# Block inverses in two pairs of groups with one transpose in, and a gated feed-forward whose norm factor is applied at the PSUM read

## The chip, the cores and the metric

One Trainium2 chip, one of its cores, one launch. The metric is the device time of that launch in microseconds (us). The core has TensorE (PE) for matrix products, VectorE (DVE), ScalarE (ACT), GpSimd (POOL) and SyncE (SP, which here only issues DMAs). All data is float32; products are done in float32 or, for the large weights, as three products of rounded parts (below).

## The reference, cut to what matters

256 tokens of width 1024 pass through two layers of a first block and one layer of a second one. A layer of the first block is

```python
x = x + 0.5 * swiglu(rms_norm(x, ffn1_norm[l]), ffn1_w_in[l], ffn1_w_out[l])
... mixer: forgetting attention, RWKV-7, block attention, then mix_w_out
... cross attention to a memory
x = x + 0.5 * swiglu(rms_norm(x, ffn2_norm[l]), ffn2_w_in[l], ffn2_w_out[l])

def rms_norm(t, g):  y = t * rsqrt(mean(t * t, -1) + 1e-6);  return y * g
def swiglu(h, w_in, w_out):
    gate, up = split(h @ w_in, 2, -1);  return (silu(gate) * up) @ w_out
```

with w_in 1024 x 5632 and w_out 2816 x 1024. So there are four gated feed-forwards. The factor rsqrt(...) is one number a token, the gain g one a feature.

RWKV-7 and, in the second block, the gated delta rule (GDN, 8 heads, two directions, chunks of 64 tokens) each need the inverse of unit triangular 64 x 64 matrices: 16 units of 128 rows (two matrices each) at a time, once in each layer's RWKV and once in each of GDN's four quarters (direction x half of the heads). In GDN the 64 x 64 inverses are joined to the units that the scan uses.

## The kernel before, in words

**Stages.** The kernel is a row of blocks; each engine has its own program in a block, and all meet at its end. Activations lie feature-major: tile k of 8 holds 128 features by 256 tokens.

**Slabs.** Weights come in slabs of 1 MB (8 x 128 rows by 256 columns) through a ring of three places; SP issues a slab's DMA when the slab three before it is no longer needed (`load_slabs`, L267). `Split` (L326 to L379) makes a rounded part `slab_hi` on ACT (L354) and the rest `slab_lo` on POOL (L363), in three places each: ACT may start slab i when PE is done with slab i-3; POOL follows ACT; PE waits for `slab_lo`. `product3` (L382) then gives hi x hi, hi x lo and lo x hi, so that a slab is 48 matmuls of 256 columns.

**Feed-forward** (`ffn_stage`, L519). The norm (`Norm`, L440) comes first: ACT squares x (L464), PE sums over features with a matrix of ones, 8 float32 matmuls (L484), ACT takes the root as Ln and Exp (L470, L472; each loads a table), DVE makes h = x * gain * rstd (L491), ACT and DVE split h (L420, L426), and only then PE starts on slab 0. Meanwhile PE runs four idle products (`keep_busy`, L433). In the first feed-forward of a layer the gain comes by a DMA that SP issues behind the first three slabs (`LayerParams`, L781). Then 11 pairs of slabs: slab 2i gives 256 gate columns into one bank, slab 2i+1 the up columns into another; ACT applies Silu out of PSUM (L555), DVE multiplies with the up bank (L593), ACT and DVE split the product (L558, L426). Before w_out (12 slabs, L502) PE waits for the last product, since its first sums go to banks 0 and 1, which the last pair (i = 10) also uses.

```python
for jj in range(4):
    if jj >= 2:
        pe.wait_ge(x_updated, 2 * (jj - 1))
    ... K.bank[2 * (jj % 2) + j]
```

**Inverse** (`BlockSolve` L1192, `Inverse` L1279). DVE turns the 32-row diagonal strips of the matrices with four transposes, each of 32 partitions by 512 (L1219), inverts 16 x 16 blocks on all partitions at once (L1222 to L1248), ACT widens the result for X (L1266, four instructions) while POOL widens it for its transpose xt (L1269, four), DVE turns both back (L1253, 1024 columns each). Then two levels join 16-blocks to 32 and 64: with M the masked part (POOL, L1326), T = M X (PE), T is copied to SBUF (ACT, L1395), U = xt T and V = T xt (PE), X -= U, xt -= V (DVE, L1409, L1410). The 16 units go in four groups of 4 units (256 columns); groups 0 and 1 run all their levels, then groups 2 and 3, each group of a pair with two banks (U goes over T). In GDN a third level joins the halves (L1355, L1371, L1414, L1415). ACT copies the diagonal blocks of each group before the solve (L1383).

**GDN** (`gdn_stages`, L2922). In quarter q the inverse of q and the scan of q-1 are interleaved by hand: scan steps 0 to 3 with the matrices, 4 to 7 with the solve, step 8 + pair ahead of each pair of inverse steps (six pairs).

## Time and profile before

| | us |
|---|---|
| median of 3 runs | 2930.77 (2929.78 to 2937.19) |
| the profiled execution | 2935.89 |
| its span | 2934.0 |
| mean granted TensorE clock of it | 0.888 |

| engine | busy, share of the span |
|---|---|
| PE | 2444.5 (83%) |
| DVE | 1165.4 (40%) |
| ACT | 1122.3 (38%) |
| POOL | 1242.2 (42%) |

An engine's busy share says how much of the span its instructions cover; matmuls overlap, so that PE's share is not its share of peak. What a stage costs is read from the waits inside it: who is idle, and what ends the idle time. The granted clock is 1.0 at 2.4 GHz and 0.5 at 1.2 GHz.

### The profile page before, as it was taken

How to read it: one execution, taken by the hardware profiler on the slowest of the kernel's cores; microseconds unless marked ns; L12 is line 12 of the kernel's file. 1: busy time of each engine (PE TensorE's matmuls, PEld its weight loads, DVE VectorE, ACT ScalarE, POOL GpSimd, SP SyncE). 2: the span in 40 equal slices, each digit the busy share in tenths (PEclk: the TensorE clock that was granted, in tenths of full speed). 3: DMA queues.
4: the chain of work that ended last, by engine and by line, in shares of the span. 5: the costliest groups of instructions: out<-in, count | busy, mean ns of one | idle time of the engine just before them, and what ended most of it. 6: DMA issues, size and time to landing. Idle time of an engine off the chain costs nothing. (4 is left out here: it accounts for less than half of the span.)

```text
span 2934.0 us, 42793 instructions
## 1 busy us (share of the span) xinstructions
PE 2444.5 (83%) x18163; PEld 2122.1 (72%) x18163; DVE 1165.4 (40%) x2067; ACT 1122.3 (38%) x1495; POOL 1242.2 (42%) x356
## 2 busy tenths in 40 slices
PE   5998968877898998977967899699957776887878
PEld 4997845375898998854456799567746556787878
DVE  2112664332210111665242211266756664334990
ACT  4433422434442443322334443456832221533333
POOL 2874510051775775610033577332211110774655
PEclk8999968987999999977987999899967777898998
DMA  4554401431553553500333354321000000553432
GB/s 138 187 175 123 144 1 44 132 125 46 172 180 124 171 182 118 173 29 12 121 113 101 110 180 143 126 76 58 29 1 1 1 1 17 171 172 115 143 123 94
DMA packets 298691, 305.98 MB, mean 104 GB/s; under 512 B 7249, under 2 KB 294461, under 8 KB 298493
## 3 DMA queue, kind: packets, MB, share of 16 engines
q1 hardware_dynamic: 298493, 303.16, 32.1%
q8 instruction: 146, 2.39, 0.4%
q14 instruction: 52, 0.43, 0.0%
HBM read 302.09 MB, written 1.05 MB: 103 GB/s over the span
## 5 line engine op out<-in xcount | busy, mean ns | idle before, releaser
L363 POOL TENSOR_TENSOR slab_lo<-ring,slab_hi 128x2048 fp32r<-128x2048 f32 (+1 forms) x242 | 1096.5, 4540 | 1045.8 <-ACT slab_hi L354 1045.8
L354 ACT CAST slab_hi<-ring 128x2048 fp32r<-128x2048 f32 (+1 forms) x242 | 451.1, 1868 | 639.8 <-PE bank L386 573.4
L384 PE MATMUL bank<-ffn_h_hi,slab_hi 128*128 128x256 f32 x1408 | 403.1, 286 | 24.0 <-DVE ffn_h_lo L426 24.0
L385 PE MATMUL bank<-ffn_h_lo,slab_hi 128*128 128x256 f32 x1408 | 402.2, 286 | 0.0
L386 PE MATMUL bank<-ffn_h_hi,slab_lo 128*128 128x256 f32 x1408 | 402.1, 286 | 0.0
L384 PEld LDWEIGHTS bank<-ffn_h_hi,slab_hi 128*128 128x128 f32 x1408 | 274.5, 195 | 27.2 <-issue 27.2
L385 PEld LDWEIGHTS bank<-ffn_h_lo,slab_hi 128*128 128x128 f32 x1408 | 274.4, 195 | 0.0
L386 PEld LDWEIGHTS bank<-ffn_h_hi,slab_lo 128*128 128x128 f32 x1408 | 274.2, 195 | 0.0
L593 DVE TENSOR_TENSOR hidden<-gate,bank 128x512 f32<-128x512 f32 x44 | 30.2, 687 | 456.8 <-PE bank L386 456.8
L384 PE MATMUL bank<-ffn_hidden_hi,slab_hi 128*128 128x256 f32 x704 | 199.6, 284 | 3.3 <-DVE hidden L593 3.3
L385 PE MATMUL bank<-ffn_hidden_lo,slab_hi 128*128 128x256 f32 x704 | 199.2, 283 | 0.0
L386 PE MATMUL bank<-ffn_hidden_hi,slab_lo 128*128 128x256 f32 x704 | 199.2, 283 | 0.0
L1326 POOL TENSOR_TENSOR inv_m<-inv_d,const 128x256 f32<-128x256 f32 x48 | 34.4, 733 | 324.3 <-ACT inv_d L1383 273.1
L2259 POOL TENSOR_TENSOR tile_lo<-ring,tile_hi 128x1024 fp32r<-128x1024 f32 (+1 forms) x38 | 87.6, 2310 | 189.3 <-ACT tile_hi L2252 189.3
L384 PEld LDWEIGHTS bank<-ffn_hidden_hi,slab_hi 128*128 128x128 f32 x704 | 135.1, 192 | 4.2 <-DVE hidden L593 4.2
L386 PEld LDWEIGHTS bank<-ffn_hidden_hi,slab_lo 128*128 128x128 f32 x704 | 135.1, 192 | 0.0
L385 PEld LDWEIGHTS bank<-ffn_hidden_lo,slab_hi 128*128 128x128 f32 x704 | 135.1, 192 | 0.0
L384 PE MATMUL bank<-fh_hi,slab_hi 128*128 128x256 f32 x352 | 103.6, 294 | 32.4 <-POOL slab_lo L363 18.5
L3233 DVE SCALAR_TENSOR_TENSOR fcon<-fraw,prm,fcon 128x256 f32<-128x256 f32 x88 | 126.5, 1498 | 0.8
L2270 PE MATMUL bank<-both_hi,tile_hi 128*128 128x512 f32 (+2 forms) x296 | 107.8, 380 | 21.3 <-ACT tile_hi L2252 21.3
L385 PE MATMUL bank<-fh_lo,slab_hi 128*128 128x256 f32 x352 | 102.9, 292 | 0.0
L1668 PE MATMUL bank<-ring,cs 128*2 128x256 f32 x384 | 102.8, 394 | 0.0
(570 smaller groups left out, 5847.8 us busy)
## 6 DMA issues: line engine op xcount, KB each, us to landing
ring<-in_ffn_w_in SPq DMA_DIRECT2D x88, 1024.0 KB, 5.1
ring<-in_ffn_w_out SPq DMA_DIRECT2D x32, 1024.0 KB, 5.0
ring<-in_w_in SPq DMA_DIRECT2D x30, 1024.0 KB, 5.3
ring<-in_mix_w_in SPq DMA_DIRECT2D x24, 1024.0 KB, 5.4
...
```

What stands on the lines that cost most here:

```text
L354: act.copy(self.hi[i % self.PLACES][:, 0:w], K.ring[n % RING][:, 0:w]).then_inc(self.hi_ready, 1)
L363: pool.tensor_tensor(self.lo[i % self.PLACES][:, 0:w], place[:, 0:w], self.hi[i % self.PLACES][:, 0:w].bitcast(F32), ALU.subtract).then_in ...
L384: pe.matmul(out, w[0], act[0], start=start, stop=False)
L385: pe.matmul(out, w[0], act[1], start=False, stop=False)
L386: return pe.matmul(out, w[1], act[0], start=False, stop=stop)
L593: dve.tensor_tensor(whole_hidden[:, i % 2, :], gate[:, i % 2, :], K.bank[2 * (i % 2) + 1][:, :], ALU.mult).then_inc(product_ready, 1)
L1326: pool.tensor_tensor(self.mask[s][l % 2][:, :, :], self.diag[g][:, :, :], level, ALU.mult)\
L1668: last = pe.matmul(K.bank[self.BANKS[self.n % 2]][0:2, 0:HALF], K.cs[:, self.k, :], self.w[:, self.k, :], start=(self.k == 0), stop=(self. ...
L2259: last = pool.tensor_tensor(self.lo[u % self.PLACES][:, :, dst], self.source(u)[:, :, src], self.hi[u % self.PLACES][:, :, dst].bitcast(F3 ...
L2270: pe.matmul(out, hi[:, k, 0:m], both.hi[:, k, 0:tokens], start=(k == 0), stop=False)
L3233: last = dve.scalar_tensor_tensor(o[:, q, :], r[:, q, j:j + T], tap, o[:, q, :], ALU.mult, ALU.add)
```

## The change

Feed-forward: PE no longer waits for the norm. The parts are made from x * gain (without rstd), the sum of squares is built on DVE (squares of all 2048 columns, then three additions) and summed over partitions by one matmul after the second slab, and rstd is multiplied in when DVE reads the gate and up banks. PE starts on `slab_hi` alone and takes the `slab_lo` products after the others of the first half. The first gain DMA goes ahead of the slabs, with a tile of its own. POOL starts when all of x's parts are there. w_out's first sums go to banks 2 and 3 (in the convolutional feed-forward too).

```diff
+def feature_major_late(pe, split, bank, w, act, first=None):
+
+    for j in range(2):
+        out, col = bank[:, j * T:(j + 1) * T], slice(j * P, (j + 1) * P)
+        for k in range(KD):
+            if first is not None and j == 0:
+                first(k)
+            pe.matmul(out, w[0][:, k, col], act[0][:, k, :], start=(k == 0), stop=False)
+            pe.matmul(out, w[0][:, k, col], act[1][:, k, :], start=False, stop=False)
+        if j == 0:
+            split.wait_rest(pe)
+        for k in range(KD):
+            last = pe.matmul(out, w[1][:, k, col], act[0][:, k, :], start=False, stop=(k == KD - 1))
     return last
...
-def ffn_out_pe(K, pe, split, hidden, x_updated):
+def out_bank(jj, j):
+    return 2 * ((jj + 1) % 2) + j
+
+
+def ffn_out_pe(K, pe, split, hidden, x_updated, other_banks):
 
     for jj in range(4):
+        if jj == 1:
+            other_banks()
         if jj >= 2:
...
+    def act_parts(self, act):
+        for k in range(KD):
+            last = act.activation(self.parts.hi[:, k, :], self.x[:, k, :], ACT.Copy, scale=self.gain[:, k:k + 1])
+            if k % 2:
+                last.then_inc(self.parts.hi_ready, 1)
+
+    def act_root(self, act):
+        K = self.K
+        act.wait_ge(self.squared_summed_root, 2)
+        K.act_own.after(act, act.activation(self.rstd[:, :], self.bank[:, 0:T], ACT.Ln, bias=K.c("eps"), scale=1.0 / D))
+        act.activation(self.rstd[:, :], self.rstd[:, :], ACT.Exp, scale=-0.5).then_inc(self.squared_summed_root, 1)
+
+    def dve_parts(self, dve):
+        for k in range(KD):
+            if k % 2 == 0:
+                dve.wait_ge(self.parts.hi_ready, k // 2 + 1)
+            last = dve.scalar_tensor_tensor(self.parts.lo[:, k, :], self.x[:, k, :], self.gain[:, k:k + 1],
+                                            self.parts.hi[:, k, :].bitcast(F32), ALU.mult, ALU.subtract)
+            if k % 2:
+                last.then_inc(self.parts.lo_ready, 1)
+
+    def dve_squares(self, dve):
+
+        sq, own = self.K.h, self.K.dve_own
+        own.after(dve, dve.tensor_tensor(sq[:, :, :], self.x[:, :, :], self.x[:, :, :], ALU.mult))
+        for n in (4, 2):
+            own.after(dve, dve.tensor_tensor(sq[:, 0:n, :], sq[:, 0:n, :], sq[:, n:2 * n, :], ALU.add))
+        dve.tensor_tensor(sq[:, 0, :], sq[:, 0, :], sq[:, 1, :], ALU.add).then_inc(self.squared_summed_root, 1)
+
+    def pe(self, pe):
+        pe.wait_ge(self.squared_summed_root, 1)
+        pe.matmul(self.bank[:, 0:T], self.K.c("ones"), self.K.h[:, 0, :], start=True, stop=True).then_inc(self.squared_summed_root, 1)
...
             def _(pool):
+                pool.wait_ge(parts.lo_ready, KD // 2)
...
             def _(act):
-                norm.act(act, between=lambda: split.act(act, 2))
+                if params is not None:
+                    act.wait_ge(params.first_ready, 1)
+                else:
+                    split.act(act, 1)
+                norm.act_parts(act)
+                split.act(act, 3)
+                norm.act_root(act)
                 for i in range(N):
                     split.act(act, 2 * i + 4)
-                    K.wait_slabs(act, n0 + 2 * i + 1)
-                    if i >= 2:
-                        act.wait_ge(product_ready, i - 1)
-                    act.activation(gate[:, i % 2, :], K.bank[2 * (i % 2)][:, :], ACT.Silu).then_inc(silu_ready, 1)
+                    act.wait_ge(gate_ready, i + 1)
+                    act.activation(gate[:, i % 2, :, :], gate[:, i % 2, :, :], ACT.Silu).then_inc(silu_ready, 1)
                     split.act(act, 2 * i + 5)
                     act.wait_ge(product_ready, i + 1)
-                    act.copy(flat(hidden.hi[:, pair_of(i), :]), whole_hidden[:, i % 2, :]).then_inc(hidden.hi_ready, 1)
+                    hidden.act(act, pair_of(i), whole_hidden[:, i % 2, :, :])
...
-                norm.pe(pe)
                 if params is not None:
                     params.pe_first(pe)
-                keep_busy(K, pe, K.bank[5], 4)
+                keep_busy(K, pe, K.bank[4], 3)
...
                     for part in range(2):
-                        w = split.next_view(pe)
+                        w = split.next_rounded(pe)
                         if i >= 2:
                             pe.wait_ge(product_ready, i - 1)
-                        K.slab_done(feature_major3(pe, K.bank[2 * (i % 2) + part], w, (parts.hi, parts.lo), KD, HALF,
-                                                   first=(lambda k: pe.wait_ge(parts.lo_ready, k // 2 + 1))
-                                                   if i == part == 0 else None))
-                pe.wait_ge(product_ready, N)
-                ffn_out_pe(K, pe, split, hidden, x_updated)
+                        K.slab_done(feature_major_late(pe, split, K.bank[2 * (i % 2) + part], w, (parts.hi, parts.lo),
+                                                       first=(lambda k: pe.wait_ge(parts.lo_ready, k // 2 + 1))
+                                                       if i == part == 0 else None))
+                    if i == 0:
+                        norm.pe(pe)
+                pe.wait_ge(product_ready, N - 1)
+                ffn_out_pe(K, pe, split, hidden, x_updated, lambda: pe.wait_ge(product_ready, N))
...
                 if params is not None:
                     params.dve_first(dve)
-                norm.dve(dve)
+                norm.dve_parts(dve)
+                norm.dve_squares(dve)
+                dve.wait_ge(norm.squared_summed_root, 3)
...
                     if i < N:
+                        K.wait_slabs(dve, n0 + 2 * i + 1)
+                        if i >= 2:
+                            dve.wait_ge(product_ready, i - 1)
+                        dve.tensor_tensor(gate[:, i % 2, :, :], pair(2 * (i % 2)), norm.all_tokens(2), ALU.mult)\
+                            .then_inc(gate_ready, 1)
+                    if i >= 1:
+                        hidden.dve(dve, pair_of(i - 1), whole_hidden[:, (i - 1) % 2, :, :])
+                    if i < N:
+                        K.wait_slabs(dve, n0 + 2 * i + 2)
+                        if i >= 1:
+                            dve.wait_ge(product_ready, i)
+                        K.dve_own.after(dve, dve.tensor_tensor(up[:, :, :], pair(2 * (i % 2) + 1), norm.all_tokens(2),
+                                                               ALU.mult))
                         dve.wait_ge(silu_ready, i + 1)
-                        K.wait_slabs(dve, n0 + 2 * i + 2)
                         if i >= 2:
                             dve.wait_ge(hidden.lo_ready, i - 1)
-                        dve.tensor_tensor(whole_hidden[:, i % 2, :], gate[:, i % 2, :],
-                                          K.bank[2 * (i % 2) + 1][:, :], ALU.mult).then_inc(product_ready, 1)
-                    if i >= 1:
-                        hidden.dve(dve, pair_of(i - 1),
-                                   whole_hidden[:, (i - 1) % 2, :].rearrange("p (a t) -> p a t", a=2))
+                        dve.tensor_tensor(whole_hidden[:, i % 2, :, :], up[:, :, :], gate[:, i % 2, :, :], ALU.mult)\
+                            .then_inc(product_ready, 1)
```

`LayerParams.sync_first` issues the first gain DMA, `dve_first` now signals `first_ready`; `wait_rest` waits for `lo_ready` of the slab that `next_rounded` gave.

Inverse: ACT gathers the diagonal strips of each group into one 128 x 512 tile (`compact`), which DVE turns with one transpose; DVE widens for X, ACT for xt, POOL no longer takes part in that. The levels run over two pairs of groups (8 units, 512 columns), one level of each in turn, with three banks each; T1 and `compact` share space with the widened tiles.

```diff
+    def act_compact(self, act, g):
+
+        for i, rows in enumerate(self.GROUPS):
+            act.copy(self.p.compact[rows, 4 * g:4 * g + 4, :], self.lt[rows, 4 * g:4 * g + 4, 32 * i:32 * i + 32])\
+                .then_inc(self.compacted, 1)
...
-        for g, rows in enumerate(self.GROUPS):
-            src = self.lt[rows, :, 32 * g:32 * g + 32].rearrange("p u (b c) -> p c b u", b=2)
-            last = dve.transpose(p.turned[rows, :, :], src)
-        K.dve_own.after(dve, last)
+        dve.wait_ge(self.compacted, 16)
+        K.dve_own.after(dve, dve.transpose(p.turned[:, :, :], p.compact.rearrange("p u (b c) -> p c b u", b=2)))
...
+    def dve_out(self, dve):
+
+        K = self.K
+        dve.wait_ge(self.solved, 1)
+        K.dve_own.after(dve, self.widen(0, lambda out, src, scale: dve.tensor_scalar(out, src, scale, None, ALU.mult)))
+        for i, dst in enumerate(self.targets):
+            if i:
+                dve.wait_ge(self.widened, 1)
+            dve.transpose(dst[:, :, :].rearrange("p u (b c) -> p c b u", b=4),
+                          self.p.wide[i].rearrange("p c a r -> p (c a) r")).then_inc(self.x_ready, 1)
 
     def act(self, act):
-        self.widen(act, 0, lambda out, src, scale: act.activation(out, src, ACT.Copy, scale=scale))
-
-    def pool(self, pool):
-        self.widen(pool, 1, lambda out, src, scale: pool.tensor_scalar(out, src, scale, None, ALU.mult))
+
+        act.wait_ge(self.solved, 1)
+        self.widen(1, lambda out, src, scale: act.activation(out, src, ACT.Copy, scale=scale)).then_inc(self.widened, 1)
...
+        bank = K.bank[bank:bank + 6]
+        self.t_bank, self.u_bank, self.v_bank = bank[0:2], bank[2:4], bank[4:6]
...
+        self.steps = [(p, l) for l in self.levels for p in range(2)]
...
+    def pe_second(self, pe, i):
+        p, l = self.steps[i]
+        pe.wait_ge(self.t_copied, i + 1)
+        pe.wait_ge(self.x_ready, 2 if i < 2 else 2 + i - 1)
+        if l != self.JOIN:
+            if l != self.levels[-1]:
+                self.blocks(pe, self.u_bank[p], self.xt(p), self.T1[p])
+            last = self.blocks(pe, self.v_bank[p], self.T1[p], self.xt(p))
+        else:
+            src, dst = self.joined()
+            for q in range(8):
+                last = pe.matmul(self.v_bank[p][src, q * CH:(q + 1) * CH], self.T1[p][dst, q, :],
+                                 self.xt(p)[dst, q, :], start=True, stop=True)
+        last.then_inc(self.uv_ready, 1)
+
+    def pe(self, pe, between=lambda i: None):
+
+        self.pe_first(pe, 0)
+        self.pe_first(pe, 1)
+        for i in range(0, len(self.steps), 2):
+            for step in (i, i + 1):
+                self.pe_second(pe, step)
+                between(step)
+            if i + 2 < len(self.steps):
+                self.pe_first(pe, i + 2)
+                self.pe_first(pe, i + 3)
...
+            act.copy(self.diag[half, 4 * g:4 * g + 4, :], self.lt[half, 4 * g:4 * g + 4, half]).then_inc(self.d_ready, 1)
+        self.solve.act_compact(act, g)
```

With eight units an instruction, `blocks` issues 16 matmuls instead of 8, and ACT's and DVE's instructions have 512 columns instead of 256; POOL makes four masks of 512 columns instead of eight of 256 (RWKV and GDN). `gdn_stages` is unchanged, but `between` is now called after each of the six second halves, so scan step 8 + i stands behind U and V of inverse step i. In the scan, the product for the new state goes to bank 0 and the output to bank 1 alone, with a wait of the fourth output for the copy of the third.

## Rows read from the trace of the kernel before

**Rows 1.** The page: TensorE's granted clock in 40 equal slices of the span, in tenths.

```profile
PEclk8999968987999999977987999899967777898998
```

**Rows 2.** Busy time by stretch (from:to, length, PE, PEld, DVE, ACT, POOL, clock, DMA share, GB/s).

```profile
36.20:56.80 20.60, 12.56 (x25) 7.37 (x26) 6.56 (x12) 11.95 (x15) 8.97 (x2) 0.67 0.70 224
56.80:186.40 129.60, 129.58 (x1057) 129.46 (x1057) 15.06 (x23) 53.79 (x44) 100.62 (x22) 0.98 0.54 174
725.00:741.80 16.80, 7.15 (x24) 4.48 (x24) 7.47 (x10) 11.76 (x15) 8.99 (x2) 0.80 0.34 109
...
409.50:426.70 17.20, 0.00 (x0) 0.00 (x0) 12.62 (x27) 3.37 (x6) 3.63 (x4) 0.50 0.00 0
426.70:440.90 14.20, 12.89 (x320) 12.02 (x320) 6.48 (x14) 2.98 (x8) 2.90 (x4) 0.84 0.01 3
...
2185.50:2207.00 21.50, 18.45 (x448) 17.20 (x448) 10.44 (x25) 7.48 (x20) 2.87 (x4) 0.90 0.01 3
...
2312.00:2336.50 24.50, 7.38 (x32) 6.31 (x32) 17.93 (x45) 2.82 (x7) 6.11 (x7) 0.57 0.00 0
2336.50:2366.00 29.50, 26.98 (x504) 25.00 (x504) 15.31 (x40) 8.75 (x22) 2.95 (x4) 0.89 0.01 2
```

**Rows 3.** ACT in order of time, second feed-forward of layer 0: start, length, operation.

```profile
727.10 3.68 ACT L354 CAST slab_hi<-ring 128x2048 fp32r<-128x2048 f32 x2
...
732.09 0.47 ACT L470 ACTIVATE rstd<-bank,const 128x256 f32<-128x256 f32 x1
732.58 1.28 ACT L472 ACT_TABLE_LOAD   x1
733.88 0.42 ACT L472 ACTIVATE rstd<-rstd 128x256 f32<-128x256 f32 x1
```

**Rows 4.** PE in order of time there; then the first gain in the first feed-forward.

```profile
725.68 3.72 PE L484 MATMUL bank<-h,const 128*128 128x256 f32 x16 [2.36 <-ACT h L464]
729.24 3.60 PE L433 MATMUL bank<-const 128*128 128x512 f32 x8
741.85 0.55 PE L384 MATMUL bank<-ffn_h_hi,slab_hi 128*128 128x256 f32 x1 [9.01 <-DVE ffn_h_lo L426]
...
47.63 0.27 PE L827 MATMUL bank<-const,param_rows 8*128 8x8 f32 x1 [4.42 <-DMA param_rows<-in_ffn_norm]
```

**Rows 5.** Small DMAs of the mixer (L962, L964), issue to landing.

```profile
DMA to landing us min/median/max: 2.5/2.6/2.9
```

**Rows 6.** POOL and DVE in order of time, there; last, the first feed-forward's same product.

```profile
762.99 4.62 POOL L363 TENSOR_TENSOR slab_lo<-ring,slab_hi 128x2048 fp32r<-128x2048 f32 x1 [1.13 <-ACT slab_hi L354]
...
741.02 2.48 DVE L426 TENSOR_TENSOR ffn_h_lo<-h,ffn_h_hi 128x512 fp32r<-128x512 f32 x4
...
766.79 0.69 DVE L593 TENSOR_TENSOR hidden<-gate,bank 128x512 f32<-128x512 f32 x1 [10.83 <-PE bank L386]
...
82.79 0.69 DVE L593 TENSOR_TENSOR hidden<-gate,bank 128x512 f32<-128x512 f32 x1 [10.83 <-PE bank L386]
```

**Rows 7.** DVE, POOL and PE at the turn from w_in to w_out, first feed-forward.

```profile
188.58 3.59 DVE L426 TENSOR_TENSOR ffn_hidden_lo<-hidden,ffn_hidden_hi 128x512 fp32r<-128x512 f32 x1 [0.66 <-ACT ffn_hidden_hi L558]
...
188.10 3.52 POOL L363 TENSOR_TENSOR slab_lo<-ring,slab_hi 128x1536 fp32r<-128x1536 f32 x1 [0.73 <-ACT slab_hi L354]
...
187.30 0.39 PE L384 MATMUL bank<-ffn_hidden_hi,slab_hi 128*128 128x256 f32 x1 [0.84 <-DVE hidden L593]
```

**Rows 8.** DVE and ACT in the first GDN quarter's solve and first level.

```profile
2168.26 4.16 DVE L1219 STREAM_TRANSPOSE sol_turned<-ring 32x512 f32<-32x512 f32 x4
2172.45 0.35 DVE L1222 TENSOR_SCALAR sol_coef<-sol_turned,const 128x256 f32<-128x256 f32 x1
...
2183.48 1.93 DVE L1253 STREAM_TRANSPOSE inv_x<-sol_wide 128x1024 f32<-128x1024 f32 x1 [3.76 <-POOL sol_wide L1269]
...
2168.26 0.83 ACT L1383 COPY inv_d<-ring 64x256 f32<-64x256 f32 x2 [2.69 <-DVE ring L2784]
2179.76 2.57 ACT L1266 ACTIVATE sol_wide<-sol_solved,const 128x256 f32<-128x256 f32 x4 [10.67 <-DVE sol_solved L1248]
```

221 lines of the change are left out of this document (104 added, 117 removed).

## The prediction

> **What bounds the kernel now.** I first read the page's slices of the granted clock [rows 1]: they dip where the serial stages are, so I looked at both parts of the change by stretch [rows 2]. In the steady part of a feed-forward the reader is to see that PE is busy through 129.58 of 129.60 us at clock 0.98: 1057 matmuls, 22 slabs at about 5.8 us. POOL has 100.62 of work there, 4.62 a slab, with an idle 1.13 before it that ends by ACT's `slab_hi` [rows 6]. So PE is the bound there, and nothing that DVE, ACT or POOL do inside it is worth time. The heads are another matter. From 725.00 to 741.80 the first real matmul does not start [rows 2, 4]: it waits for the chain squares, sum, root, h, parts. In the first feed-forward of a layer the head is 20.60, because the gain lands 11.4 us after the start (47.63 less 36.20, PE waiting 4.42 for it) [rows 4]. At the turn to w_out PE waits 0.84 for the last product [rows 7].
>
> For the inverses I took the two pieces of a stage apart [rows 2, 8]: a serial solve in which PE has no matmul (409.50 to 426.70), and the levels after it, which go by latency from engine to engine (14.20 for 320 matmuls of 64 columns at RWKV, 21.50 for 448 in GDN's quarter 0, 24.50 and 29.50 with the scan woven in).
>
> **Feed-forward head, second of a layer (twice).** Times from the stage's start. Before, slab 3's product begins at 41.8 (766.79 less 725.00) [rows 6]. After:
> ACT rounds slab 0 (1.9, half of 3.68 [rows 3]), then eight parts of 256 columns at 0.42, the price of the 256-column Exp [rows 3]: to 5.2. DVE follows each with 0.62 (a quarter of 2.48 [rows 6]), so it ends at 5.8. PE can start at 3.6 on `slab_hi` and be through 16 matmuls by about 6.
> POOL now waits for the last part: slab 0's rest from 5.8 + squares. DVE's squares of 2048 columns cost 4 x 0.62 less three starts, 2.2; they read SBUF twice, as the addition at 188.58 did that took 3.59 instead of some 0.7, ending 0.55 after POOL's (188.10 + 3.52) [rows 7]. That row reads as one of the two standing still until the other is done. I take it that whoever begins first goes first, and that DVE does, since it is already there when the wait is satisfied: squares 5.8 to 8.0, POOL 8.0 to 12.6; then DVE's additions, 1024, 512 and 256 columns (1.2, 0.62, 0.35 at the same rates [rows 6, 8]), each fall in turn with a whole split of POOL: 12.6 to 13.8, split to 18.4; to 19.0, split to 23.6; to 24.0. The sum of squares comes at about 24, and the matmul after slab 1 waits for it little or not at all: slab 0 has 32 matmuls left, 3.9 us at full clock (0.12 each [rows 2]) and 7.0 at half (0.22, half of 3.60/8 [rows 4]). I take 5.6, the clock rising on the way: 12.6 to 18.2, slab 1 to 24.0. Slab 2 is behind the sum in PE's queue and goes from 24.4 to 30.2. ACT's root is 0.47 + 1.28 + 0.42 [rows 3], to 26.6. Slab 3's rounding stands behind the root on ACT: to 28.5, POOL's rest to 33.1. PE begins slab 3 at 30.2, has its 16 matmuls of `slab_hi` done at 32.1, waits 1.0 for `slab_lo`, and does the other 32 by 36.9. Before: 41.8. Gain 4.9, twice: 9.8.
>
> If exclusion did not exist, the sum would come at 5.8 + 2.2 + 2.2 = 10.2 and slab 3 would not be late: 3 us more in each of four. If the heads were eaten up by low clock and waiting, nothing of them would stay. Both ends stand in the rivals. The squares could also take nothing from POOL; the value between is the row's.
>
> The Trainium skill bears on this ("SBUF — State Buffer", section "SBUF: two separate sides"): DVE with two SBUF operands and GpSimd share a port pair as an exclusive lock, held for a whole instruction. It speaks against this change, which replaces reads from PSUM by SBUF pairs. By it the sum's chain is as I have it; without it, 3 us a feed-forward faster. The trace agrees with 3.59 for a 0.7 us addition.
>
> **First feed-forward of a layer (twice).** The gain's DMA now goes first: small DMAs land 2.5 to 2.9 after issue [rows 5], so transposed and copied by 3.2; parts to 6.5 and 7.0. Slab 0 is 1 MB, 4.7 us at this head's 224 GB/s [rows 2], and lands at about 6.5; it is rounded by 8.4 while DVE squares, 7.0 to 9.2. POOL: 9.2 to 13.8. The same chain then gives the last addition at 25.2, the root's end at 27.8, slab 3 rounded at 29.7, split at 34.3, done at 38.2. Before: 46.6 (82.79 less 36.20 [rows 6]). Gain 8.4, twice: 16.8.
>
> **Steady part and turn.** DVE gets two instructions of 512 columns more a pair (0.69 each [rows 6]) and loses none, on an engine with 15.06 busy of 129.60 [rows 2]: zero. `up` x `gate` (two from SBUF) and the parts' subtraction may fall against POOL's splits; POOL's spare 1.13 a slab [rows 6] covers one blocked instruction of 0.69. ACT's Silu reads SBUF: zero. If that cover were gone, POOL would set the slab; see rival C. At the turn PE no longer waits for the last product: 0.84 saved [rows 7], four times, 3.4; then jj = 1 waits for it three slabs later, when it is long done. Convolutional feed-forward: the same banks, but its product is ready earlier than its slab: zero, at most 0.84.
> Feed-forwards: 9.8 + 16.8 + 3.4 = 30.0.
>
> **Inverse in RWKV (twice).** Four transposes of 4.16 together [rows 8] become one of 128 x 512: half of the 1.93 of 1024 columns [rows 8], 1.0; minus 3.1. But ACT's gather is new: four copies of 32 x 128 elements a group. A copy of 64 x 256 is 0.42 (0.83/2 [rows 8]); I take 0.32, nearer to it than to nothing (ends 0.2 and 0.42). The last group's diagonals (0.83) and its four copies (1.3) now stand ahead of the transpose: plus 2.1. Net minus 1.0. Widening: the last of POOL's four is waited for 3.76 [rows 8]; DVE itself needs 4 x 0.35 + 0.05 [rows 8]: minus 2.3. ACT's four take 2.57 [rows 8] beside DVE's own 1.45 + 1.93 and are done first. Levels: 14.20 [rows 2] had eight steps of 8 + 16 matmuls in chains of four hand-overs; now four steps of twice the size, U and V to their own banks so that PE need not wait between them. 320 matmuls at 12.89 busy leave 1.3 idle; with that gone: 12.7, minus 1.5. Bounds: the same 14.2 (longer copies and subtractions of 512 columns, each 0.3 more, in the path), and 11.0 if the clock of 0.84 goes to 0.98. Taken minus 1.3. Sum 4.6, twice: 9.2.
>
> **Inverse in GDN (four quarters).** Quarter 0: the matrices end just ahead of the copies (ACT idle 2.69 until DVE's `ring` [rows 8]), and they come faster than the 2.1 that a group now takes on ACT. So the last two groups' work, 4.1, stands ahead of the transpose, against minus 3.1: net plus 1.0. Widening minus 2.3. Levels and join: 21.50 with 18.45 busy [rows 2]: to the busy time, minus 3.1. Gain 4.4. Quarters 1 to 3: the scan's copies are beside the gather on ACT and I add 0.85, two copies: plus 1.85; widening minus 2.1 (the scan's own update sits there); levels 29.50 with 26.98 busy [rows 2], and `between` is called after each half, so that a scan step fills each wait that remains: the idle 2.5 goes, and 1.4 more by a clock that rises from 0.89 to 0.94 over 27 busy us: minus 3.9. Bounds for each: 0 and minus 6. Gain 4.15, three times 12.4. GDN: 16.8.
>
> **Sum.** 30.0 + 9.2 + 16.8 = 56.0. The profiled execution took 2935.9 (span 2934.0), 5.1 above the median of 2930.8. So 2880 for a run like it, 2875 as a median. Under 0.3% (9 us) a difference would count as none.
>
> **Rivals.**
> A, the exclusion costs less: the sum is ready at 10.2, slab 3 in time, 3 us more in each feed-forward: 12 us, 2863. For it: L593, one operand in PSUM, keeps its 0.69 beside POOL [rows 6]. Against: 188.58 [rows 7]. 0.12.
> B, the heads give nothing: PE's head is spent at half clock and in waits for `slab_lo` at 0.22 a matmul; what starts early ends at the same time, since POOL's first split is at 8 and the sum late. 26.6 less gained: 2901. For it: clock 0.67 and 0.80 in these heads [rows 2]. 0.17.
> D, the inverse's gains are halved by the gather on ACT and longer instructions: 13 less: 2888. For it: 0.83 for two small copies [rows 8]. 0.12.
> C, slower. The steady part becomes POOL's. Each slab's split now meets one or two blocked DVE instructions, and the chain `slab_hi`, split, free place runs without slack: 1.9 + 4.62 + one blocked 0.7 is 7.2 in the worst case against 5.75, with three places the mean over POOL alone is 4.62 + two times 0.69 = 6.0, or 6.9 when `slab_hi` cannot run ahead. At 6.9, 1.1 x 88 slabs = 97, less 56: 2972. It decides from 0.64 us a slab (56/88). Against it: POOL's idle of 1.13 [rows 6] and ACT's 53.79 of 129.60 [rows 2], so ACT is ahead. 0.05.
>
> **How the numbers follow.** Forecast 0.54 (2875), A 0.12, D 0.12, B 0.17, C 0.05. The likeliest one's own width is 2865 to 2885, the bounds of the inverses' terms. To leave out no more than 2 in 10 the range takes in A and D and reaches B: 2858 to 2902. Faster 0.93 (all but C and a B with the inverses at nothing, 2927), same 0.02, slower 0.05.
>
> **What would show it.** First feed-forward: the first real matmul at about 3.6 to 7 after the start instead of 20.6, slab 3's product read at 38, and in the second at 37. DVE's three additions with times of over 4 us, and the sum's matmul at 24: if they take 1.2, 0.6 and 0.4, exclusion is not what I think (A). PE's idle time before `slab_lo` of slab 3, ended by POOL. In the steady part PE busy as before and POOL idle over 0.4 a slab; PE waits for `slab_lo` in each slab would be C. Inverses: one transpose of 1.0, four widenings on DVE of 0.35, levels 12.7 and 18.4. I am wrong if the heads gain under 2 us each, or if the RWKV levels are not shorter.

## The result, and the profile after

The changed kernel takes 2889.23 us (median of 4, 2883.84 to 2890.84) where the kernel before took 2932.02; the ratio is 0.9846, with the interval 0.9833 to 0.9859. So it is 42.8 us faster. The forecast was 2875, 56 us faster, with 2858 to 2902 as its range. In a later comparison on one chip the changed kernel took 2885.53 against 2931.59, with the same ratio, 46 us faster.

The profiled execution took 2883.84, span 2881.8, 52.2 less than the span before. The page's clock line first, to be held against [rows 1]:

```profile
PEclk8999967997999999977987999899967777999989
```

Then busy time by stretch, columns as in [rows 2]: the first feed-forward's head and steady part, the second one's head, the levels of the first RWKV, the levels of GDN's first quarter, and the matrices ahead of them.

```profile
35.30:55.90 20.60, 15.07 (x80) 11.91 (x81) 17.07 (x14) 10.30 (x12) 11.69 (x3) 0.77 0.66 208
56.80:186.40 129.60, 127.49 (x1059) 127.03 (x1059) 60.36 (x46) 58.70 (x49) 107.94 (x24) 1.00 0.59 190
713.40:725.00 11.60, 5.74 (x22) 3.20 (x22) 8.80 (x10) 9.99 (x12) 5.47 (x1) 0.95 0.01 2
...
415.42:428.47 13.05, 11.86 (x320) 11.58 (x320) 5.66 (x7) 2.35 (x4) 2.53 (x2) 0.82 0.02 4
2145.60:2167.60 22.00, 17.52 (x448) 17.03 (x448) 11.17 (x14) 6.10 (x11) 2.54 (x2) 0.81 0.01 2
2102.24:2133.50 31.26, 26.51 (x64) 15.11 (x64) 12.68 (x32) 9.51 (x27) 1.27 (x1) 0.51 0.00 1
```

The first head has 80 matmuls in its 20.60 us where it had 25. DVE's busy time in the first feed-forward's steady part is 60.36 instead of 15.06, and PE is busy for 127.49 us all the same. The 2.1 us left are two waits of PE: 1.1 for slab 3's `slab_lo` and, by this line, 1.0 for the sum of squares:

```profile
59.83 0.48 PE L594 MATMUL bank<-h,const 128*128 128x256 f32 x1 [0.99 <-DVE h L590]
```

The two rows of levels are cut at other instructions than those of [rows 2]: at PE's first matmul in RWKV, and in GDN at DVE's first transpose out. From and to the same instructions the kernel before has:

```profile
426.78:440.81 14.03, 12.89 (x320) 12.02 (x320) 6.40 (x13) 2.98 (x8) 2.90 (x4) 0.84 0.01 4
2183.50:2207.00 23.50, 18.45 (x448) 17.21 (x448) 12.44 (x26) 7.48 (x20) 2.87 (x4) 0.86 0.01 3
```

So RWKV's levels are 1.0 shorter and those of GDN's first quarter 1.5; in the latter PE still idles for 4.5 us (5.05 before), at a clock of 0.81 (0.86 before).

The second feed-forward's head on DVE, in order of time (start, length); its zero is 713.4:

```profile
716.16 3.29 DVE L579 SCALAR_TENSOR_TENSOR ffn_h_lo<-x,prm,ffn_h_hi 128x256 fp32r<-128x256 f32 x8 [3.09 <-ACT ffn_h_hi L565]
719.37 2.28 DVE L587 TENSOR_TENSOR h<-x 128x2048 f32<-128x2048 f32 x1
721.69 10.39 DVE L589 TENSOR_TENSOR h<-h 128x1024 f32<-128x1024 f32 x2
732.11 4.72 DVE L590 TENSOR_TENSOR h<-h 128x256 f32<-128x256 f32 x1
740.65 0.69 DVE L684 TENSOR_TENSOR gate<-bank,rstd 128x512 f32<-128x512 f32 x1 [3.82 <-ACT rstd L573]
```

And PE there, the lines with a wait or the sum:

```profile
717.19 0.36 PE L428 MATMUL bank<-ffn_h_hi,slab_hi 128*128 128x256 f32 x1 [0.93 <-DVE ffn_h_lo L579]
726.06 2.08 PE L433 MATMUL bank<-ffn_h_hi,slab_lo 128*128 128x256 f32 x8 [5.82 <-POOL slab_lo L363]
737.78 0.59 PE L594 MATMUL bank<-h,const 128*128 128x256 f32 x2
747.14 1.10 PE L433 MATMUL bank<-ffn_h_hi,slab_lo 128*128 128x256 f32 x7 [1.11 <-POOL slab_lo L363]
```

The squares of 2048 columns take 2.28, and the last addition, of 256 columns, takes twice that: 4.72. PE starts 3.8 after the zero (before: 16.9 [rows 4]), waits 5.82 for the first `slab_lo`, and 1.11 for slab 3's.

The inverse's answers to [rows 8], in GDN's first quarter, DVE in order of time:

```profile
2135.71 1.04 DVE L1337 STREAM_TRANSPOSE sol_turned<-sol_wide 128x512 f32<-128x512 f32 x1 [2.26 <-ACT sol_wide L1331]
...
2144.09 1.47 DVE L1379 TENSOR_SCALAR sol_wide<-sol_solved,const 128x256 f32<-128x256 f32 x4
2145.60 1.92 DVE L1383 STREAM_TRANSPOSE inv_x<-sol_wide 128x1024 f32<-128x1024 f32 x1
```

Stage lengths from one block's start to the next show where the time came from (worked out from the instructions that begin each block; the second execution of the changed kernel stands beside the first):

```
                             before   after   again
first feed-forward, layer 0  215.29  205.33  205.12
second                       211.48  206.53  206.51
first, layer 1               219.50  209.45  210.25
second                       211.47  206.52  206.56
RWKV, layer 0 (to levels)     59.48   55.79   54.94
RWKV, layer 1                 59.49   54.97   55.86
GDN, four quarters           346.53  335.46  331.95
```

Feed-forwards 29.9, RWKV 8.2, GDN 11.1, together 49.2 of 52.2. Of the rest, 1.0 lies in the convolutional feed-forward (252.89 to 251.86) and 1.7 in the block behind it (11.98 to 10.30). The new banks are not what shortened the former: `ffn_only`, which has them, took 253.00 there, and `inverse_only`, which has not, 251.31.

### The profile page after: what moved, and what is told of

The parts are those of the page before. It is cut to its first block and busy times, and to the rows that moved or that the text cites. A ratio compares the mean times of both kernels' runs of the same rounds, so it can differ in the third digit from the quotient of the medians.

```text
span 2881.8 us, 42748 instructions
## 1 busy us (share of the span) xinstructions
PE 2414.7 (84%) x18099; PEld 2099.7 (73%) x18099; DVE 1351.8 (47%) x2101; ACT 1139.7 (40%) x1543; POOL 1239.0 (43%) x308
## 5 line engine op out<-in xcount | busy, mean ns | idle before, releaser
L363 POOL TENSOR_TENSOR slab_lo<-ring,slab_hi 128x2048 fp32r<-128x2048 f32 (+1 forms) x242 | 1120.8, 4646 | 996.7 <-ACT slab_hi L354 875.7
L428 PE MATMUL bank<-ffn_h_hi,slab_hi 128*128 128x256 f32 x1408 | 350.8, 286 | 4.6 <-ACT slab_hi L354 2.5
L429 PE MATMUL bank<-ffn_h_lo,slab_hi 128*128 128x256 f32 x1408 | 348.8, 285 | 0.0
L433 PE MATMUL bank<-ffn_h_hi,slab_lo 128*128 128x256 f32 x1408 | 200.1, 285 | 20.5 <-POOL slab_lo L363 20.5
L1445 POOL TENSOR_TENSOR inv_m<-inv_d,const 128x512 f32<-128x512 f32 x24 | 30.4, 1268 | 430.5 <-ACT inv_d L1503 323.5
L433 PEld LDWEIGHTS bank<-ffn_h_hi,slab_lo 128*128 128x128 f32 x1408 | 183.0, 193 | 22.3 <-POOL slab_lo L363 22.3
L395 PE MATMUL bank<-fh_hi,slab_hi 128*128 128x256 f32 x352 | 105.5, 300 | 31.4 <-POOL slab_lo L363 15.8
L703 DVE SCALAR_TENSOR_TENSOR x<-bank,x 128x256 f32<-128x256 f32 x32 | 12.1, 420 | 221.6 <-PE bank L397 221.6
L397 PE MATMUL bank<-fh_hi,slab_lo 128*128 128x256 f32 x352 | 103.8, 295 | 0.0
```

Source lines behind the costliest of these rows:

```text
L363: pool.tensor_tensor(self.lo[i % self.PLACES][:, 0:w], place[:, 0:w], self.hi[i % self.PLACES][:, 0:w].bitcast(F32), ALU.subtract).then_in ...
L395: pe.matmul(out, w[0], act[0], start=start, stop=False)
L397: return pe.matmul(out, w[1], act[0], start=False, stop=stop)
L428: pe.matmul(out, w[0][:, k, col], act[0][:, k, :], start=(k == 0), stop=False)
L429: pe.matmul(out, w[0][:, k, col], act[1][:, k, :], start=False, stop=False)
L433: last = pe.matmul(out, w[1][:, k, col], act[0][:, k, :], start=False, stop=(k == KD - 1))
```

## The experiments

**Each part alone, and the changed kernel again.** `ffn_only` has the feed-forward's hunks, `inverse_only` the inverse's; the second counts its gather on another semaphore.

```diff
-        dve.wait_ge(self.compacted, 16)
+        dve.wait_ge(self.widened, 16)
```

> The feed-forward part of the change alone (the late norm, the first gain ahead of the slabs, w_out's banks), with the old inverses. My theory: its share of the gain is what the stages of the two traces show, 10.0 in each first feed-forward of a layer and 4.95 in each second, 1 in the convolutional one, so 30 us: 2902 where the kernel before takes 2932. Rival: the heads' gain is given back, because TensorE's clock falls elsewhere when the heads are shorter; then the stages of the feed-forwards are shorter by 30 in the trace, but the whole by under 20 (2912 and more).

> The inverse part alone (one transpose in, widening on DVE and ACT, two pairs with three banks each), with the old feed-forward; its gather is counted on the semaphore of the widening. My theory: 4 us in each RWKV stage and 11 to 18 in GDN, so 2910 to 2914. Rival: the parts overlap in what they save, through the clock, and this one alone gives under 10 us (2922 and more).

> The changed kernel once more, for a second trace. In its first trace the matrices of GDN's first quarter took 31.2 us at a granted clock of 0.51, in the kernel before 27.2 at 0.63, with the same 64 matmuls. If that belongs to the kernel (what PE did just before it), it is there again: 31 at 0.5. If it is where the chip's change of clock happened to fall in one execution, it is different this time, 27 to 31, and other stages move by one to four us in its place. Whole: 2889.

Measured on one chip, in brackets the ratio to the kernel before with its 95% interval: `ffn_only` 2902.07 (0.9907, 0.9894 to 0.992), `inverse_only` 2914.11 (0.9939, 0.992 to 0.9959), the changed kernel 2885.53, the kernel before 2931.59. That is 29.5, 17.5 and 46.1 us less: the two parts add up within the noise (the interval of `inverse_only` alone is 12 to 23 us). The second trace also settles the matrices of GDN's first quarter. There it reads:

```profile
2101.20:2128.50 27.30, 22.09 (x64) 13.29 (x64) 12.68 (x32) 8.53 (x23) 1.26 (x1) 0.64 0.00 1
```

64 matmuls in 27.3 us at clock 0.64, where the first execution of the same kernel has 31.26 us at 0.51. PE idled in waits between them in both. The 4 us belong to the execution, not to the change.

In `inverse_only` the same thing shows in two stages that no edit touched, layer 0's RWKV tail and the mixer's output. First the changed kernel's second execution, then `inverse_only`:

```profile
423.48:561.33 137.85, 125.58 (x676) 64.91 (x676) 49.01 (x151) 38.19 (x96) 0.00 (x0) 0.90 0.28 89
602.48:707.34 104.86, 76.25 (x472) 66.89 (x472) 31.36 (x81) 48.39 (x77) 36.73 (x8) 0.82 0.24 81
```

```profile
432.94:573.30 140.36, 129.42 (x676) 66.89 (x676) 49.10 (x151) 38.18 (x96) 0.00 (x0) 0.88 0.27 87
614.78:723.47 108.69, 80.20 (x472) 70.77 (x472) 31.37 (x81) 48.40 (x77) 36.72 (x8) 0.76 0.24 78
```

The counts are equal, the lengths 2.5 and 3.8 apart, the clock 0.02 and 0.06. In that same execution of `inverse_only` layer 1's pair of stages, with the same instructions, is 2.5 and 3.8 shorter than layer 0's. Its own stages are shorter by 23.7 than before's (RWKV twice 4.5, GDN 14.7), its median by 17.5.

**The sum of squares on PE.** PE sums all eight tiles of squares in the stretch in which it waited for the first `slab_lo`.

```diff
         if j == 0:
+            if between is not None:
+                between()
             split.wait_rest(pe)
...
-        own.after(dve, dve.tensor_tensor(sq[:, :, :], self.x[:, :, :], self.x[:, :, :], ALU.mult))
-        for n in (4, 2):
-            own.after(dve, dve.tensor_tensor(sq[:, 0:n, :], sq[:, 0:n, :], sq[:, n:2 * n, :], ALU.add))
-        dve.tensor_tensor(sq[:, 0, :], sq[:, 0, :], sq[:, 1, :], ALU.add).then_inc(self.squared_summed_root, 1)
+        dve.tensor_tensor(sq[:, :, :], self.x[:, :, :], self.x[:, :, :], ALU.mult).then_inc(self.squared_summed_root, 1)
...
-        pe.matmul(self.bank[:, 0:T], self.K.c("ones"), self.K.h[:, 0, :], start=True, stop=True).then_inc(self.squared_summed_root, 1)
+        for k in range(KD):
+            last = pe.matmul(self.bank[:, 0:T], self.K.c("ones"), self.K.h[:, k, :], start=(k == 0), stop=(k == KD - 1))
+        last.then_inc(self.squared_summed_root, 1)
```

> The changed kernel, but DVE makes the squares only, and PE sums them over features and partitions with eight float32 matmuls that stand between slab 0's products of slab_hi and those of slab_lo, where PE was idle from 720.24 to 726.06. The three additions that each waited for a whole split of POOL go, the root comes some 11 us earlier, and slab 3 is rounded in time. My theory (exclusion of DVE and POOL set the chain, and the idle stretch cost clock too): 1.1 us of wait at slab 3 goes, and the 6.8 us at half clock in slabs 0 and 1 go with it, up to 3.4: 3 to 4.5 us in each of four feed-forwards, so 2871 to 2877. Rival: the clock stays as it was and only the wait at slab 3 goes: 4 us in all, 2885. Other rival: the eight matmuls at half clock take over 5.8 us and hold up slab 0: no gain or a loss.

Measured: 2869.74 (0.9806, 0.9788 to 0.9823), 15.8 less than the changed kernel. PE in order of time, the second feed-forward of layer 0 (zero 707.6):

```profile
711.40 0.35 PE L428 MATMUL bank<-ffn_h_hi,slab_hi 128*128 128x256 f32 x1 [0.93 <-DVE ffn_h_lo L581]
715.91 3.72 PE L594 MATMUL bank<-h,const 128*128 128x256 f32 x16 [1.47 <-DVE h L589]
720.29 1.22 PE L435 MATMUL bank<-ffn_h_hi,slab_lo 128*128 128x256 f32 x8 [0.66 <-POOL slab_lo L363]
```

The eight (the view counts 16) fit: 0.66 of the wait is left. The four stages are 2.4, 3.8, 3.3 and 3.1 shorter than in the changed kernel's second execution. Of the second stage's 3.8, 1.4 is slab 3's wait, 0.4 the matmul and its hand-over after slab 1, and 2.0 slab 0, whose remaining matmuls now run at the higher level behind a PE that was not idle (the first eight take 1.22 us instead of 2.08). My theory held on size (3 to 4.5 a stage expected, one stage fell short of it).

**The additions without POOL.**

```diff
-                pool.wait_ge(parts.lo_ready, KD // 2)
+                pool.wait_ge(norm.squared_summed_root, 1)
```

> The changed kernel, but POOL waits for DVE's last addition and not only for the last part. In the changed kernel the three additions of a head took 5.4, 4.96 and 4.7 us, each ending with a split of POOL. My theory: with POOL not yet started they take 1.2, 0.65 and 0.4, the sum is ready at about 12.5 after the stage's start instead of 25, slab 3 no longer waits; but POOL's first split ends 2.3 later, so slab 0 does too: slab 4 begins within 1 us of where it did, and the whole is 0 to 4 us slower than the changed kernel (2886 to 2890). Rival: the additions' times are their own (over 4 us each), POOL starts 15 us later in each head, and the kernel is 50 us slower.

Measured: 2900.1 (2 runs), 11 to 15 slower than the changed kernel, where 0 to 4 was expected. DVE and PE in order of time, the second feed-forward:

```profile
728.63 1.95 DVE L589 TENSOR_TENSOR h<-h 128x1024 f32<-128x1024 f32 x2
730.62 0.42 DVE L590 TENSOR_TENSOR h<-h 128x256 f32<-128x256 f32 x1
...
735.67 2.08 PE L433 MATMUL bank<-ffn_h_hi,slab_lo 128*128 128x256 f32 x8 [8.48 <-POOL slab_lo L363]
757.06 1.21 PE L433 MATMUL bank<-ffn_h_hi,slab_lo 128*128 128x256 f32 x8 [1.10 <-POOL slab_lo L363]
```

and ACT's root there:

```profile
748.34 0.48 ACT L572 ACTIVATE rstd<-bank,const 128x256 f32<-128x256 f32 x1 [17.97 <-PE bank L594]
```

The lengths are as the theory has them: 1.95 for two additions that took 10.39, 0.42 for the one that took 4.72. But the wait at slab 3 is still there, 1.10. The root waited 17.97 for PE although the additions had ended at 731.0: the sum's matmul stands behind slab 1 in PE's queue, and slab 3's rounding stands behind the root. So an early sum gives nothing while its matmul stays there, and the first `slab_lo`, later by 2.7, makes a second feed-forward 3.0 longer (209.49 against 206.51). My theory had slab 4 begin within 1 us of where it did; it begins 3.0 later. In a layer's first feed-forward PE's wait of 0.99 for the sum is gone, but in layer 0's the first `slab_lo` comes 2.6 later too, and that stage is 3.0 longer.

**The gain behind the slabs.**

```diff
-                if params is not None:
-                    params.sync_first(sync)
                 K.load_slabs(sync, n0 + RING)
                 if params is not None:
+                    params.sync_first(sync)
                     params.sync(sync)
```

> The changed kernel with the first gain's DMA issued behind the first three slabs again, as before the change. My theory: the parts of a layer's first feed-forward begin some 8 us later, and everything of the head with them: 7 to 8.5 us in each of two stages, so 2901 to 2903, and of the 10 us that each of these stages gained 2 are left. Rival: the chain of additions sets the head's end and takes up part of the delay: under 4 us each (2894 and less).

Measured: 2913.44 (2 runs). PE's first lines in the first feed-forward, whose block starts at 35.4:

```profile
47.04 0.27 PE L933 MATMUL bank<-const,first_rows 8*128 8x8 f32 x1 [23.34 <-DMA first_rows<-in_ffn_norm]
```

in the changed kernel, with its block from 35.6:

```profile
37.52 0.27 PE L934 MATMUL bank<-const,first_rows 8*128 8x8 f32 x1 [13.59 <-DMA first_rows<-in_ffn_norm]
```

The transpose that waits for the gain begins 11.7 after the start instead of 1.9, and the two stages take 216.4 and 220.2: 11.3 and 10.0 longer, where 7 to 8.5 was expected, and longer than in the kernel before (215.3, 219.5). So of what these two stages gained nothing is left without the DMA's place in the queue. That does not make the DMA alone worth 10 us. With the old order of work its worth was not tried; in the kernel before, a second feed-forward, which has its gain from the start, was only 3.8 shorter than layer 0's first (211.48 against 215.29; 5.0 from block end to block end), so an estimate for the DMA alone is 4 to 5 us, and the rest needs both edits. The whole kernel is 27.9 slower than the changed one, 6.6 more than the two stages: in its trace the RWKV tails and the mixer's outputs of both layers have the longer of the two lengths seen above. Whether the edit has a part in that is open.

**A small DVE instruction.**

```diff
+                        K.dve_own.after(dve, dve.tensor_tensor(extra[:, :], K.x[:, 0, 0:16], norm.rstd[:, 0:16], ALU.mult))
```

> The changed kernel with one more DVE instruction in each of a feed-forward's 11 pairs: x times rstd over 128 x 16 elements, both from SBUF, its result unused. It tells how near DVE is to setting the time of the steady part. In the trace a pair's four DVE instructions take 0.69 and 4.4 and 0.69 and 4.4 us of a pair's 11.5, the two long ones because they read twice from SBUF and wait for a split of POOL to end. My theory: the small one, alone some 0.1, waits for a whole split too, 4.6; a pair then needs 14.8 of DVE, 3.3 more than PE, so the kernel gets 100 to 145 us slower (2985 to 3030). Rival (the long times are only how the profile shows overlapping, or are set by the amount of data): 0.1 us each, hidden, 2886. Between them: it slips into POOL's idle time in part, 20 to 50 us.

Measured: 2880.7 (2 runs). DVE in order of time:

```profile
92.39 4.60 DVE L700 TENSOR_TENSOR extra<-x,rstd 128x16 f32<-128x16 f32 x1
...
102.72 4.40 DVE L698 TENSOR_TENSOR hidden<-up,gate 128x512 f32<-128x512 f32 x1
107.04 0.16 DVE L700 TENSOR_TENSOR extra<-x,rstd 128x16 f32<-128x16 f32 x1
107.24 0.69 DVE L685 TENSOR_TENSOR gate<-bank,rstd 128x512 f32<-128x512 f32 x1
107.85 0.68 DVE L453 TENSOR_TENSOR ffn_hidden_lo<-hidden,ffn_hidden_hi 128x512 fp32r<-128x512 f32 x1
```

and POOL:

```profile
87.30 19.27 POOL L363 TENSOR_TENSOR slab_lo<-ring,slab_hi 128x2048 fp32r<-128x2048 f32 x4 [3.08 <-ACT slab_hi L354]
109.66 4.62 POOL L363 TENSOR_TENSOR slab_lo<-ring,slab_hi 128x2048 fp32r<-128x2048 f32 x1 [3.09 <-ACT slab_hi L354]
```

The same 16 columns take 4.60 us inside POOL's splits (87.30 to 106.57) and 0.16 in POOL's idle time behind them; all 44 take 160 to 4606 ns, median 3494. So the waiting is real and its length is POOL's. What I concluded from it was wrong: w_in is no longer than without the instruction (in layer 0's second feed-forward 141.3 us from the stage's start to w_out's first matmul, 141.4 in the changed kernel). It is not free either. In each feed-forward PE now waits in w_out for the last pair's parts, which DVE makes behind the added instruction; in layer 0's second one:

```profile
866.04 0.39 PE L395 MATMUL bank<-ffn_hidden_hi,slab_hi 128*128 128x256 f32 x1 [0.85 <-DVE ffn_hidden_lo L453]
```

The time of 2880.7 hides this, because the tile that the instruction writes makes w_out faster by itself (below). Against `pad_only`, which has the tile and not the instruction, the four feed-forwards are 5.7 us longer, 3.1 of it these waits. Where one instruction waits through a split, those behind it find POOL idle (107.85: 0.68 instead of 4.4), so that DVE does not add up a whole split for each of them. That the two pairs of banks let a product be late is my reading; no run tried it.

The Trainium skill says of this ("SBUF — State Buffer", section "SBUF: two separate sides") that the port pair of DVE and GpSimd is an exclusive lock, held for the whole instruction, and that the loser fully blocks. The trace agrees: 4.60 against 0.16.

**The gather: back to four transposes, or on POOL.**

```diff
-        dve.wait_ge(self.compacted, 16)
-        K.dve_own.after(dve, dve.transpose(p.turned[:, :, :], p.compact.rearrange("p u (b c) -> p c b u", b=2)))
+        for g, rows in enumerate(self.GROUPS):
+            src = self.lt[rows, :, 32 * g:32 * g + 32].rearrange("p u (b c) -> p c b u", b=2)
+            last = dve.transpose(p.turned[rows, :, :], src)
+        K.dve_own.after(dve, last)
```

> The changed kernel with DVE's four transposes of 32 x 512 in again and without ACT's gather. From the matrices' end to the end of the transposes in, the kernel before took 4.2 us in all four GDN quarters, the changed one 3.3 in the first and 6.15 in the others, where ACT has scan steps 4 to 7 ahead of the last two groups' copies. My theory: 4.2 in all again, that is 0.9 more, then 1.9 less three times, and 0.25 more in each RWKV: 4.3 us faster than the changed kernel, about 2882. Rival: the wait for ACT is hidden behind what follows and nothing changes (2886).

```diff
     def pool(self, pool):
+        for g in range(4):
+            self.before(pool, g)
+            self.solve.pool_compact(pool, g)
+        pool.wait_ge(self.solve.compacted, 16)
         for i, (p, l) in enumerate(self.steps[0:4]):
...
-        self.solve.act_compact(act, g)
```

> The changed kernel with the gather of the strips on POOL, which is idle there, instead of ACT. My theory: from the matrices' end to the turned strips it takes four copies of some 0.35 and the transpose of 1.04 and hand-overs, 2.6 us, in every quarter, instead of 3.3 and three times 6.15; with 0.8 less in each RWKV that is 13 us faster than the changed kernel, about 2873. Rival: POOL's copies of 32 partitions take 0.8 each, as its masks of 128 x 512 take 1.27: 4.3 to the turned strips, and 4 us in all (2882).

Measured: 2878.35 (2 runs) and 2881.15 (4 runs, 0.9824, 0.9794 to 0.9853). The phases of GDN, worked out from DVE's instructions in each trace, in us:

```
                       before  after  again  four tr.  POOL
q0 matrices             27.25  31.21  27.14   28.82   27.24
   to strips turned      4.19   3.30   4.46    4.21    2.55
   solve, widening      11.07   8.84   8.85    8.85    9.72
   levels and join      23.46  21.97  22.72   22.25   21.95
q1 matrices             26.75  25.50  23.91   26.23   25.65
   to strips turned      4.26   6.15   6.13    4.27    2.55
   solve, widening      17.21  15.90  15.89   15.88   16.77
   levels               27.11  22.56  22.70   22.23   22.32
q2 matrices             29.74  32.99  33.05   32.97   32.98
   to strips turned      4.25   6.16   6.13    4.24    2.57
   solve, widening      18.31  15.83  15.82   16.11   16.60
   levels and join      31.25  28.12  28.18   29.27   29.27
q3 matrices             25.53  25.50  25.50   25.73   26.33
   to strips turned      4.26   6.16   6.13    4.28    2.55
   solve, widening      18.32  15.82  15.81   15.82   16.61
   levels               27.85  22.78  22.83   22.02   22.76
last scan               45.71  46.68  46.71   50.11   46.66
sum                    346.53 335.46 331.95  333.31  325.07
```

"To strips turned" is as expected in both. But of the four transposes' 5.6 in q1 to q3 nothing is left in the stage: 1.7 and 2.3 more in two stretches of matrices, 3.4 in the last scan. POOL's gather keeps 6.9 of 12.6. In the whole kernel neither is told apart from the changed one (ratio 0.9846): 7.2 us less from two runs, and 4.4 less where 13 was expected. One thing that it gives back can be read: DVE's second instruction of the solve, in q1 of `pool_gather`,

```profile
2200.07 1.36 DVE L1340 SCALAR_TENSOR_TENSOR sol_coef<-sol_turned,const,sol_coef 128x256 f32<-128x256 f32 x1
```

and in the changed kernel:

```profile
2199.65 0.48 DVE L1340 SCALAR_TENSOR_TENSOR sol_coef<-sol_turned,const,sol_coef 128x256 f32<-128x256 f32 x1
```

POOL's masks now run there (2198.57, 2.59 us), and DVE waits for one of them: the 0.8 to 0.9 more in each "solve, widening". In RWKV the strips are turned 0.75 sooner and the solve takes 0.87 longer, so that nothing is gained (55.00, 55.87).

**64 bytes.** `extra_small` came out faster than it should, by 2.5 us in each of three w_out parts. `pad_only` keeps its tile and not the instruction.

```diff
         up = K.sb("up", [P, 2, T], ctx=ctx)
+        extra = K.sb("extra", [P, 16], ctx=ctx)
```

> The changed kernel with the tile of 128 x 16 that the small instruction wrote, but without the instruction: all tiles of a feed-forward allocated behind it lie 64 bytes further on a partition. In the kernel with the instruction w_out's slabs went at 5.44 us instead of 5.76, 2.5 us less in each of three feed-forwards. If the addresses do that, the pace is 5.44 here too, the kernel 8 to 10 us faster than the changed one (2877). If what DVE and POOL did in time did it, the pace is 5.76 and the time 2886.

`best3` has this tile, the sum on PE and POOL's gather:

> The version that the runs point to: the changed kernel with the sum of squares on PE inside slab 0, the strips gathered by POOL instead of ACT, and the tile of 64 bytes. Feed-forward heads 12.8 us shorter (as measured), GDN 6.9 shorter, and 8 to 10 if the tile alone gives w_out's faster pace. Effects that add up: 2869.7 less 5 to 7, so 2863 to 2865 without the tile's effect and about 2855 with it. Rival: a shorter head or GDN is given back by lower clocks in stages that were not touched, as single executions showed for stages of 100 us and more (up to 4 us each): 2870.

`pad_between` is `best3` with the tile in another place:

```diff
         up = K.sb("up", [P, 2, T], ctx=ctx)
-        extra = K.sb("extra", [P, 16], ctx=ctx)
         parts = Parts(K, ctx, tag + "_h", KD)
         norm = LateNorm(K, ctx, tag, K.x, gain, parts, K.bank[5])
+        extra = K.sb("extra", [P, 16], ctx=ctx)
         split = Split(K, ctx, tag, n0, FK + 12)
```

> The kernel with the sum on PE, POOL's gather and the 64 bytes, but the 64 bytes stand between the parts of x and the slabs' parts instead of ahead of both. In the kernel with 64 bytes ahead of both, w_out's slabs (weights moved by 64 bytes against the hidden parts) went at 5.46 us, and w_in's (weights and x's parts moved alike) at 5.76 as ever. If the distance between the weights and the moving operand sets the pace, w_in's 22 slabs go at 5.46 too now: 0.3 x 22 x 4 = 26 us less, about 2826. If the weights' own address does, and w_out alone is open to it, or the hidden parts' place does, w_in stays at 5.76 and the time at 2850.

Measured: `pad_only` 2868.77 (0.9791, 0.9774 to 0.9808), `best3` 2851.9 (0.9729, 0.9713 to 0.9746), `pad_between` 2831.63 (0.9663, 0.9641 to 0.9684), 101 us less than the kernel before. `pad_only` is 17 us faster than the changed kernel, where 8 to 10 was expected: all four w_out parts go at 5.44 us a slab, and the four stages are 14.0 shorter than in the changed kernel's first execution. `best3` came out 3 below what the sum of its parts gave (about 2855). `pad_between` was to give 26 us more and gave 20. Busy time in 50 us of w_in and 40 us of w_out in layer 0's second feed-forward, PE busy throughout; the changed kernel:

```profile
781.80:831.80 50.00, 50.00 (x419) 50.00 (x418) 13.27 (x17) 20.35 (x18) 41.55 (x10) 1.00 0.59 190
861.80:901.80 40.00, 40.00 (x335) 40.00 (x334) 1.51 (x4) 13.37 (x8) 31.63 (x8) 1.00 0.51 164
```

`pad_only`:

```profile
779.90:829.90 50.00, 50.00 (x419) 50.00 (x418) 13.19 (x17) 20.26 (x18) 41.56 (x10) 1.00 0.59 190
859.90:899.90 40.00, 40.00 (x356) 40.00 (x355) 2.27 (x6) 14.54 (x9) 34.05 (x8) 1.00 0.51 164
```

`pad_between`:

```profile
772.00:822.00 50.00, 50.00 (x444) 50.00 (x443) 15.89 (x18) 21.89 (x18) 42.68 (x10) 1.00 0.60 196
852.00:892.00 40.00, 40.00 (x356) 40.00 (x355) 1.51 (x4) 10.60 (x6) 29.01 (x8) 1.00 0.36 119
```

The counts tell it: at clock 1.00 in all, 419 matmuls or 444, 335 or 356. With the tile ahead of x's parts and the weights' parts only w_out is faster; with it between them both are. What moved in both faster cases is the weights against the moving operand. It is not the whole of it: in `pad_between` the feed-forward that opens layer 0 goes at 5.65 a slab throughout, that of layer 1 at 5.65 for a few slabs and then at 5.44, with the same addresses. And in `extra_small`, with the addresses of `pad_only`, the first w_out goes at 5.44 up to PE's wait in its third slab and at 5.65 from there to its end, while the other three go at 5.44 on both sides of that wait. So the pace is not the addresses' alone: it changed at a short wait of PE in one of four. What else sets it stays open.

## Why the prediction was right, point by point

**Bound and head.** PE was the bound of the steady part and stayed it; rival C did not occur. One step about it was wrong and cost nothing: I let POOL stand still for a DVE instruction of 0.69, and mostly it is DVE that stands still for a split, 4.4 us at a time, which is why its busy time there went from 15.06 to 60.36 and POOL's only from 100.62 to 107.94. The head's steps stand as forecast, counted from 713.4: the first matmul 3.8 (forecast 3.6), the first `slab_lo` 12.7 (12.6), the sum's matmul 24.4 (24.4), the root's end 27.2 (26.6), slab 3's `slab_lo` 33.7 (33.1) after a wait of 1.11 (1.0). The DVE additions wait for POOL as taken from one row [rows 7], which `extra_small` and `adds_first` confirmed.

**Terms.** The second feed-forwards gained 4.95 each (4.9 + 0.84 forecast), the first ones 10.0 (8.4 + 0.84), all four 29.9 (30.0), and `ffn_only` 29.5 as a median. That the sum fits so closely is luck: the second ones gave 0.8 less than forecast and the first ones 0.8 more. In the second, slab 0's remaining matmuls took 6.0 us where I had 5.6, and slab 3 took 7.1 where I had 6.7. PE's wait at the turn is gone as forecast. Without the early DMA nothing of the first ones' 10 is left (`gain_behind`). RWKV: 3.7 and 4.5 (4.6 each): its strips are turned 0.9 sooner (1.0 forecast), its widening is 2.2 shorter (2.3), its levels 1.0 (1.3).

**The term that was mis-sized: GDN,** 11.1 and 14.6 us in two executions, against 16.8. Its parts were: to the strips turned 0.9 less and 0.3 more in q0 (1.0 more forecast), 1.9 more in the others (1.85); widening 2.2 less (2.3) and 1.3 to 2.5 less (2.1); levels of q0 1.5 and 0.7 less (3.1). In q1 to q3 the levels gave 12.8 together (11.7), but 3.3 of it comes back in q2's matrices and 1.0 in the last scan: my reading is that what scan steps no longer do beside the levels they do elsewhere, which no run tested. I had counted the levels' stretch as if nothing were moved out of it. In the first execution 4.0 more went to q0's matrices at clock 0.51, which is that execution's. Why q0's levels do not come down to PE's busy time was only argued (longer copies and subtractions of 512 columns), and no run tried it.

**From one execution to a median.** The forecast for the profiled execution was 56.0 less; the two profiled executions of the changed kernel have spans 52.2 and 57.1 less. As a median it is 42.8 and 46. I had subtracted 5.1 because the profiled execution of before was slow by that. The changed kernel's profiled executions were its fastest, 5 to 7 below their medians, so the step from execution to median was wrong: 5.1 below where it was 5.4 above, and these 10.5 are the larger part of the 14 us between 2875 and 2889. So the range held and the forecast's own width (2865 to 2885) did not: 2889.23 lies outside it, beside the 2888 of rival D, whose mechanism did not occur. The spread comes with stages at another clock, as the two pairs of rows under `inverse_only` show.

**The rivals.** A said that with a sum ready at 10.2 slab 3 would be in time. That was wrong as a mechanism, and so was my sentence that the chain's lateness made slab 3 late: with the additions unhindered (`adds_first`) slab 3 waits as long, because the sum's matmul stands behind slab 1. Moving the matmul and leaving the additions out (`sum_on_pe`) gave 15.8, a gain of A's size (12), but in the stage read above half of it comes from slab 0's matmuls at the higher clock level, which A did not have. Only in a layer's first feed-forward did PE wait for the sum at all, 0.99. B did not occur: the heads gave 26 us in the stages. D is near the inverse's median alone, 17.5 of 26.0, but not by its mechanism; the gather took what was forecast.
